# The scan of a two-block model: one predicated copy joins the decay exponents of both directions, and the order of work around it changes

## What is computed

```python
def segsum_exp(a):                       # a: dt * A, along the tokens of a chunk
    cs = jnp.cumsum(a, axis=-1)
    diff = cs[..., :, None] - cs[..., None, :]
    return jnp.exp(jnp.where(tril, diff, -jnp.inf))

def ssd_scan(x, dt, a, b, c):            # one direction
    xdt = x * dt
    cb = einsum(c, b)                    # per group, 128 x 128 per chunk
    y_diag = einsum(cb, segsum_exp(a_dt), xdt)
    ...                                  # states, carried to the next chunk
    return y_diag + y_off

y = y_fwd + y_bwd + xs * d_skip
u = y * silu(z)                          # then an rms norm per group, and a projection
```

## Time and profile before

| | |
|---|---|
| median of 3 runs | 942.24 us (942.22 to 942.31) |
| profiled execution | 942.23 us, span 940.4 us |
| TensorE matmul, weight loads | 99%, 86% of the span |
| VectorE, ScalarE, GpSimd | 70%, 54%, 6% |
| HBM read | 164.57 MB |

### The profile page before, as it was taken

The page is one execution under the profiler, slowest core; times in us unless marked ns, Lnnn a source line. Parts: engine busy times, 40 slices in busy tenths (PEclk is TensorE's granted clock), DMA queues, the critical chain, the costliest instruction groups (busy, mean ns, idle before and its releaser), DMA issues.

```text
span 940.4 us, 13246 instructions
## 1 busy us (share of the span) xinstructions
PE 932.4 (99%) x5362; PEld 807.9 (86%) x5362; DVE 662.4 (70%) x946; ACT 507.6 (54%) x664; POOL 60.8 (6%) x68
## 2 busy tenths in 40 slices
PE   9999999999999999999999999999999999999998
PEld 8988899988888888888888888899888898888887
DVE  6779789998878764778776446767665758776433
ACT  6457876676555733456554335755653455554331
POOL 1000000023321000000003310000000000000000
PEclk9999999999999999999999999999999999999999
DMA  8943233554224475435447955353355435546551
GB/s 306 341 168 124 93 133 135 180 167 169 91 90 157 140 307 197 169 131 221 179 180 236 256 196 206 136 205 128 123 217 179 179 135 217 187 179 224 178 179 45
DMA packets 25278, 166.51 MB, mean 177 GB/s; under 512 B 2987, under 2 KB 3115, under 8 KB 6657
## 3 DMA queue, kind: packets, MB, share of 16 engines
q1 hardware_dynamic: 22464, 156.12, 46.1%
q0 software_dynamic: 2752, 9.54, 3.5%
HBM read 164.57 MB, written 1.08 MB: 176 GB/s over the span
## 4 chain that ended last, share of the span: by engine, by line
PE 86%; DVE 11%; ACT 2%; issue 1%; ACTq 0%; DVEq 0%
PE ps L393 54%; PE ps L582 11%; PE ps L587 6%; DVE conv_acc L1688 5%; DVE w_lo L1455 3%; PE ps L843 1%; PE ps L772 1%; PE ps L787 1%; PE ps L424 1%; PE ps L426 1%; PE ps L433 1%; PE ps L512 1%; PE ps L630 1%; PE ps L893 1%; PE ps L852 1%
## 5 line engine op out<-in xcount | busy, mean ns | idle before, releaser
L1455 DVE TENSOR_TENSOR w_lo<-raw,w_hi 128x2048 fp32r<-128x2048 f32 x145 | 331.3, 2291 | 181.0 <-ACT w_hi L1075 180.8
L1075 ACT ACTIVATE w_hi<-raw 128x2048 fp32r<-128x2048 f32 x145 | 275.5, 1906 | 179.1 <-PE ps L393 160.2
L393 PE MATMUL ps<-w_hi,ht 128*128 128x512 f32 (+1 forms) x576 | 181.4, 388 | 0.0
L393 PE MATMUL ps<-ht,w_hi 128*128 128x256 f32 (+1 forms) x816 | 150.6, 286 | 0.0
L393 PEld LDWEIGHTS ps<-ht,w_hi 128*128 128x128 f32 (+1 forms) x816 | 126.2, 190 | 4.1 <-issue 4.0
L393 PEld LDWEIGHTS ps<-w_hi,ht 128*128 128x128 f32 x576 | 107.3, 188 | 22.4 <-issue 1.1
L393 PE MATMUL ps<-ht,w_lo 128*128 128x256 f32 (+1 forms) x408 | 115.3, 282 | 0.0
L393 PE MATMUL ps<-w_lo,ht 128*128 128x512 f32 (+1 forms) x288 | 110.5, 384 | 0.0
L582 PE MATMUL ps<-ht,w_hi 128*128 128x512 f32 x448 | 109.5, 391 | 0.0
L393 PE MATMUL ps<-w_hi,ff_hi 128*128 128x512 f32 x256 | 99.7, 389 | 0.0
L393 PE MATMUL ps<-w_lo,ff_hi 128*128 128x512 f32 x256 | 99.6, 389 | 0.0
(11 more groups left out here) (301 smaller groups left out, 1217.4 us busy)
## 6 DMA issues: line engine op xcount, KB each, us to landing
raw<-in_w_stream SPq DMA_DIRECT2D x145, 1024.0 KB, 4.8
bias<-rel_scratch POOLq DMA_DIRECT2D x1, 3072.0 KB, 21.2
bias<-in_rpb POOLq DMA_DIRECT2D x16, 128.0 KB, 7.9
x_first<-in_x_in SPq DMA_DIRECT2D x2, 512.0 KB, 4.1
raw<-in_w_stream SPq DMA_DIRECT2D x2, 512.0 KB, 6.4
gates<-in_gate_bias POOLq DMA_DIRECT2D x4, 256.0 KB, 6.0
gates<-in_gate_bias POOLq DMA_DIRECT2D x2, 512.0 KB, 7.2
x<-in_x_in POOLq DMA_DIRECT2D x1, 1024.0 KB, 5.3
```

What stands on the lines that cost most here:

```text
L393: ins = pe.matmul(o, still, moving, start=first and n == 0, stop=last and n == 2, skip_group_check=True)
L1075: act.activation(split_home(s)[0][:, 0:width(s)], raw[s % RAW_RING][:, 0:width(s)], ACT.Copy).then_inc(hi_ready, 1)
L1455: dve.tensor_tensor(lo[:, 0:width(s)], raw[s % RAW_RING][:, 0:width(s)], hi[:, 0:width(s)].bitcast(F32), ALU.subtract).then_inc(lo_ready, 1)
```

## The change

- The matmuls with `unit` and `far` are gone. The exponents of the two directions go to banks 5 and 6 as they are. VectorE's `ssd_choose` copies bank 6 over bank 5 where a mask (`tri[:, 2]`) says so, in one `copy_predicated`. ScalarE then takes one exponential of bank 5, and `ssd_weigh` has only its multiplication left.
- The copy leaves one direction's factor on the diagonal. The other's, dt times b.c of the token itself, joins the skip term: `make_twins` multiplies b by c (4 VectorE operations in slot 28), `twin_sums` sums over the state with 16 matmuls of one column into bank 4 (slot 29), `own_terms` puts dt and `d_skip` to it, and `ssd_skip` writes x times that into its own buffer `skipped`, before y is there.
- VectorE's order in slots 28 to 36 is `scan_slot`. It splits piece s + 1 instead of s + 2 there, behind the second choice, none in slot 28; slots 37 and 38 split piece s + 1 too, and slot 39 splits 40 and 41.
- ScalarE copies the state and takes the second exponential ahead of the squares. z's chunks 2 and 3 are copied, and one silu of both is taken in slot 31. Exp's table is loaded by hand in slots 27 and 31.

```diff
-        decay_back = [at(f"decay_back{c}", [P, PER_GROUP, P], 150592 + 2048 * c) for c in range(RT)]
+        twins = [at(f"twins{i}", [P, GROUPS // 2, P], home) for i, home in enumerate((150592, 152640, 178016, 182112))]
...
+        skipped = at("skipped", [P, RT, GW], 150592)
+        own_skip = at("own_skip", [P, RT, HEADS], 158784)
...
                     pe.matmul(ps[:, 5 + d, :], cum_s[g % 2][:, 2 * c + d, :], cum_l[c][:, d, :, :],
-                              start=True, stop=False)
-                    pe.matmul(ps[:, 5 + d, :], unit[:, :], far[:, d].unsqueeze(1).to_broadcast([P, PER_GROUP, P]),
-                              start=False, stop=True).then_inc(*fill_of(key))
+                              start=True, stop=True).then_inc(*fill_of(key))
+
+            def twin_sums():
+
+                claim("twins", 4)
+                pe.wait_ge(twins_ready, 4)
+                for c in range(RT):
+                    for g in range(GROUPS):
+                        at0 = c * GROUPS + g
+                        ins = pe.matmul(ps[:, 4, at0:at0 + 1], twins[2 * c + g // 4][:, g % 4, :], tri[:, 0, P - 1:P],
+                                        start=True, stop=True)
+                ins.then_inc(*fill_of("twins"))
...
                 if 0 <= s - 28 < GROUPS:
                     ssd_decay(s - 28, 1)
+                    if s == 29:
+                        twin_sums()
...
             def decay_exps(g, c):
-                for d, dest in enumerate((decay[g % 2][c], decay_back[c])):
-                    key = ("decay", g, c, d)
-                    ready(act, key)
-                    if d == 0 and g >= 2:
-                        ready(act, ("y", g - 2))
-                    if d == 1 and g:
-                        act.wait_ge(decay_scaled, 2 * g - 1 + c)
-                    act.activation(dest[:, :, :], ps[:, 5 + d, :].rearrange("p (h l) -> p h l", h=PER_GROUP),
-                                   ACT.Exp).then_inc(*drain_of(key))
+                key = ("decay", g, c, 0)
+                emptied(act, ("decay", g, c, 1))
+                if g >= 2:
+                    ready(act, ("y", g - 2))
+                act.activation(decay[g % 2][c][:, :, :], ps[:, 5, :].rearrange("p (h l) -> p h l", h=PER_GROUP),
+                               ACT.Exp).then_inc(*drain_of(key))
...
+                if 0 <= s - 29 < GROUPS:
+                    key = ("state", s - 29)
+                    ready(act, key)
+                    act.activation(state[:, :, :], ps[:, 7, :].rearrange("p (a b) -> p a b", a=2),
+                                   ACT.Copy).then_inc(*drain_of(key))
+                if 0 <= s - 28 < GROUPS:
+                    decay_exps(s - 28, 1)
+                if s == 31:
+                    for c in (2, 3):
+                        emptied(act, ("z", c, 0)), emptied(act, ("z", c, 1))
+                    act.activation(zg_half[1][:, :, :], zg_half[1][:, :, :], ACT.Silu).then_inc(z_last_silu, 1)
+                    act.preload_act_table(ACT.Exp)
                 if 0 <= s - 30 < GROUPS:
                     g = s - 30
                     act.wait_ge(gated, g + 1)
@@ -1315,19 +1334,16 @@
                             act.wait_ge(gsq_ready, 2 * g + c)
                         act.activation(junk[:, :], xtok(c, g * GW, GW), ACT.Square,
                                        accum_out=gstat[:, 0, 2 * g + c:2 * g + c + 1]).then_inc(gsq_ready, 1)
-                if 0 <= s - 28 < GROUPS:
-                    decay_exps(s - 28, 1)
-                if 0 <= s - 29 < GROUPS:
-                    key = ("state", s - 29)
-                    ready(act, key)
-                    act.activation(state[:, :, :], ps[:, 7, :].rearrange("p (a b) -> p a b", a=2),
-                                   ACT.Copy).then_inc(*drain_of(key))
+                if s == 27:
+                    act.preload_act_table(ACT.Exp)
                 if name == "z" and closes:
+                    if chunk == 3:
+                        ready(act, "twins")
                     for r in range(RT):
                         key = ("z", chunk, r)
                         ready(act, key)
                         act.activation(zg(r, chunk * 512, 512), ps[:, bank(key), :],
-                                       ACT.Silu if chunk else ACT.Copy).then_inc(*drain_of(key))
+                                       ACT.Silu if chunk == 1 else ACT.Copy).then_inc(*drain_of(key))
...
+            def ssd_choose(g, c):
+
+                ready(dve, ("decay", g, c, 0)), ready(dve, ("decay", g, c, 1))
+                both = [ps[:, 5 + d, :].rearrange("p (h l) -> p h l", h=PER_GROUP) for d in range(2)]
+                dve.copy_predicated(both[0], tri[:, 2].bitcast(I32).unsqueeze(1).to_broadcast([P, PER_GROUP, P]),
+                                    both[1]).then_inc(*drain_of(("decay", g, c, 1)))
+
             def ssd_weigh(g, c):
 
-                emptied(dve, ("decay", g, c, 0)), emptied(dve, ("decay", g, c, 1))
-                w = decay[g % 2][c]
-                link(dve.tensor_tensor(w[:, :, :], w[:, :, :], decay_back[c][:, :, :], ALU.add))
+                emptied(dve, ("decay", g, c, 0))
                 if c == 0:
                     emptied(dve, ("cb", g))
+                w = decay[g % 2][c]
                 dve.tensor_tensor(w[:, :, :], w[:, :, :],
                                   cb[:, c, :].unsqueeze(1).to_broadcast([P, PER_GROUP, P]),
                                   ALU.mult).then_inc(decay_scaled, 1)
 
+            def make_twins():
+
+                dve.wait_ge(conv_silu, 8)
+                for c in range(RT):
+                    for half in range(2):
+                        first, tokens = 4 * half, slice(c * P, c * P + P)
+                        dve.tensor_tensor(twins[2 * c + half][:, :, :], bc[:, first:first + 4, tokens],
+                                          bc[:, GROUPS + first:GROUPS + first + 4, tokens],
+                                          ALU.mult).then_inc(twins_ready, 1)
+
+            def scan_slot(s):
+
+                g, last = s - 28, s - 29
+                if g < GROUPS:
+                    ssd_choose(g, 0)
+                    ssd_weigh(g, 0)
+                if last > 0:
+                    ssd_skip(last)
+                if g < GROUPS:
+                    ssd_choose(g, 1)
+                if last == 0:
+                    own_terms()
+                    ssd_skip(0)
+                if g == 0:
+                    make_twins()
+                else:
+                    split_lo(s + 1)
+                if g < GROUPS:
+                    ssd_weigh(g, 1)
+                if s == S_GATE + 5:
+                    dve.wait_ge(gate_bias_second, 32)
+                    gate_bias(1)
+                if last >= 0:
+                    ssd_gate(last)
+
...
+            def own_terms():
+
+                ready(dve, "twins")
+                v = own_skip[:, :, :].rearrange("p c (g h) -> p c g h", g=GROUPS)
+                for c in range(RT):
+                    ins = dve.tensor_tensor(v[:, c], dt[:, c, HEADS:2 * HEADS].rearrange("p (g h) -> p g h", g=GROUPS),
+                                            ps[:, 4, c * GROUPS:c * GROUPS + GROUPS].unsqueeze(2)
+                                            .to_broadcast([P, GROUPS, PER_GROUP]), ALU.mult)
+                ins.then_inc(*drain_of("twins"))
+                emptied(dve, "twins")
+                link(dve.tensor_tensor(own_skip[:, :, :], own_skip[:, :, :],
+                                       param("d_skip").unsqueeze(1).to_broadcast([P, RT, HEADS]), ALU.add))
+
+            def ssd_skip(g):
+
+                for c in range(RT):
+                    ins = dve.tensor_tensor(skipped[:, c, :].rearrange("p (h d) -> p h d", h=PER_GROUP),
+                                            xtok(c, g * GW, GW).rearrange("p (h d) -> p h d", h=PER_GROUP), per_head(own_skip[:, c, 4 * g:4 * g + 4], 4), ALU.mult)
+                link(ins)
+
             def ssd_gate(g):
 
                 own = xtok(all_rows, g * GW, GW)
                 ready(dve, ("y", g))
-                dve.wait_ge(x_state_ready, 2 * (g + 1))
-                for c in range(RT):
-                    v = xtok(c, g * GW, GW).rearrange("p (h d) -> p h d", h=PER_GROUP)
-                    ins = dve.tensor_tensor(v, v, per_head(param("d_skip")[:, 4 * g:4 * g + 4], 4), ALU.mult)
-                link(ins)
                 ready(dve, ("off", g))
                 for i in range(RT):
                     ins = dve.tensor_tensor(y_off[:, i].rearrange("p (h d) -> p h d", h=PER_GROUP),
                                             ps[:, 7, i * GW:i * GW + GW].rearrange("p (h d) -> p h d", h=PER_GROUP),
                                             per_head(sums[:, i, 4 * g:4 * g + 4], 4), ALU.mult)
                 ins.then_inc(*drain_of(("off", g)))
-                dve.tensor_tensor(own, ps[:, 4, :].rearrange("p (c f) -> p c f", c=2), own, ALU.add).then_inc(*drain_of(("y", g)))
```

(35 more changed lines are left out.)

5 lines of the change are left out of this document (2 added, 3 removed).

## The result

The changed kernel takes 948.29 us, the median of 9 runs (944.86 to 952.33); the kernel before took 942.27 beside it (942.14 to 943.71). The ratio is 1.0065, 95% interval 1.0046 to 1.0083: slower by 6 us. The forecast was 943.0 with a range to 947.5, so the time lies outside, above.

A forecast was written before the change was run, and what follows sets the result against it. The prediction took TensorE, busy 99% of the span at full clock, as the bound. Its terms, -7.44 + 3.4 + 1.15 - 0.68 + 4.3 = +0.73 us, put 942.23 at 943.0, range 940.9 to 947.5.

The forecast's parts named there:

- TensorE's own work: Scan slots: dropping the mask matmul 32 times saves 7.44 us; a steady slot goes from 11.31 to 10.38.
- The twins: Slot 29: 16 one-column fp32 matmuls, 32 passes priced like wider ones, add 3.4 us.
- The new wait in slot 28: TensorE waits for bank 5's exponential, held by the copy behind VectorE's split of piece 29: +1.15 us.
- The copy: VectorE's predicated copy takes 0.7 us, also beside GpSimd; bounds 0.68 and 1.21.
- rival B: Scan slots: VectorE becomes the bound, with copies of 1.21 us and slots of 11.07; 947.8 us, chance 0.22.
- list of VectorE's steps: Steady slot: copies, exponential wait, weigh, skip, split, y_off and gate sum to 2d + 8.6 to 8.7, d one copy.
- the cover: Steady slot: VectorE needs 10.1 us, under TensorE's 10.38, so TensorE still sets the pace by 0.3.
- Slot 29: No wait for y_off, by 0.3 us, so the old wait of slot 29 to 30 goes: -0.68.
- Slot 40: At its start TensorE waits for piece 40's split, queued behind gate bias, sigmoid, yt_hi and yt_lo: +4.3 us.
- Rival C: Slot 40: no wait, because the sigmoid chain ends before TensorE gets there; 938.7 us, chance 0.13.
- The sum: Whole kernel: the terms add to +0.73 us on the profiled 942.23, giving 943.0.

The follow-up runs named there:

- the last two kernels: Changed kernel, waits mended, 32-column twins in one run: 945.56 us; the same with piece 30 split in slot 29, behind the first half's product: 938.31 us.

## Why the prediction was wrong, point by point

**TensorE's own work, right.** The states of slots 30 and 31 start 10.41 us apart where 10.38 was expected: -7.44 stands. In the changed kernel:

```profile
234.40 1.02 PE L853 MATMUL ps<-x_state,btok 128*128 128x256 f32 x4
...
244.81 1.03 PE L853 MATMUL ps<-x_state,btok 128*128 128x256 f32 x4
```

**The twins, right as a price of passes (+3.4 against 3.5), and the step that failed as a whole.** The prediction wrote "Half the columns don't make a pass cheaper, so one column shouldn't either" and stopped there. It priced the time that the passes take, and put what they do to the engine's clock at nothing, without a reason: 5.1 us more in the profiled run. The cause is shown by the same passes in the kernel before (+7.7), by the same number of passes of 64 columns there (+2.9), and by the changed kernel without the twins or with them spread. It read "at the full granted clock" off the page as a fact of the kernel, when it was a fact of the work that the kernel issued.
The Trainium skill, page "TensorE: Matmul & The Clock Gate", section "What's actually happening", says that a monitor sets the clock by how busy TensorE has been. The trace agrees for the gap of slot 40; for the twins its busy row says 10.00 of 10.00 us and the clock fell, so the busy share of the profile isn't the measure by which that rule can be applied.

**The new wait in slot 28, right:** 0.99 us against 1.15.

**The copy, right:** 16 copies of 695 ns on average, against 0.7, and the one at 206.60 took 0.68 while GpSimd was at its cum_s (205.66 to 207.32). So VectorE is not the bound and the prediction's rival B is out. One entry in its list of VectorE's steps was low: the 16 products with `cb` were taken at 0.7 to 0.75 and last 0.87 on average, 1.10 where GpSimd's x_state runs beside them (289.55). The slot of 10.41 shows that the cover held.

**Slot 29, right:** no wait of more than 0.2 for y_off at full clock, in the kernel without the twins.

**Slot 40, right in place and size, incomplete in price.** TensorE waits 4.15 there against 4.3, by the chain that was named (gate bias, sigmoid, yt_hi, yt_lo, then the split at 321.69). Rival C is out. But the wait also takes the clock to half, which cost 1.7 us in the profiled run of the changed kernel and 2.5 and 2.7 in the kernels without twins and with them spread. The term put that at nothing.

**The sum.** 942.23 + 0.73 + 5.1 + 1.7 = 949.8 against 949.69 in the profiled run. In all nine runs the time less span times (1 - mean clock) is 942.6 to 943.6, around the 943.0 forecast. So the terms that were in the sum were right, and the one that was missing is larger than their balance. The chances were wrong with it: no rival lowered the clock, so the range ended at 947.5 by another mechanism, the bound on VectorE.

**Left open:** why the nine runs lose between 1.9 and 9.5 us to the clock (span times one less the mean clock) and not the same. The two fastest (944.86 and 944.89) lose 1.9, about what slot 40 alone took, so there the twins seem not to have lowered it. The kernel before is not free of this either: 6 of its 22 runs beside the first experiments took 943.6 to 943.8 with a mean clock of 0.998. Open too is whether the wait of 1.0 in slot 28, 7 us ahead of the twins, has a part in it when the twins are in one run.

## What to carry to other kernels

Price a new run of thin matmuls (few moving columns, a weight load each) twice: the time of its passes, and a possible 5 us lost to half clock behind it. Lay such passes between wide matmuls, or widen them where the passes cost no more (64 columns kept the clock here, 32 not always), and keep waits away from them, which the last two kernels suggest. When a step that saves TensorE's time shortens the slots, look also at loads that another engine issues at a fixed place in its program: here the gate-bias load became late as soon as the splits weren't.

Read the granted clock in short windows before believing a busy share: 99% busy stood on both pages, and one of the two executions took 7.5 us longer.

## What the runs showed of the hardware that was not expected

- 32 fp32 passes of one column in one run took TensorE from 2.4 to 1.2 GHz with no idle time ahead (kernel before: traced in one run, the same mean clock of 0.995 in four of four), and it stayed there 10.2 us, although wide matmuls followed without a gap. In the changed kernel with split 40 back, one run of seven kept a mean clock of 1.0. 32 passes of 64 columns did not lower it (six of six), and took no longer: both kinds start 0.11 us apart at full clock.
- 32 passes of 32 columns did so with 1.45 us of idle time directly ahead (traced in one run, mean clock 0.992 to 0.994 in five of five) and not in the profiled run without it (three of its eight runs are at 0.996).
- The half clock at the 4.1 us gap lasted 3.4 us in the changed kernel (324.3 to 327.7) and 6.8 in two kernels that differ from it elsewhere, where it set in 1.8 and 1.5 us before the gap had ended.
- A predicated copy of 128x512 fp32 with source and destination in PSUM takes 0.695 us on average over 16, as much as an add.
